# Six of eight gated head outputs turned by VectorE block transposes and a trip through DRAM, with the first output pair's last quad of inputs taken at its end

## The reference, cut to what matters

```python
o = o * lax.rsqrt(jnp.mean(jnp.square(o), axis=-1, keepdims=True) + RMS_EPS)
o = o.reshape(B, S, H * dv) * gn.astype(jnp.float32)
gate = jax.nn.silu((h @ wg).astype(jnp.float32))
return (gate * o).astype(h.dtype) @ wo
```

## Time and profile before

| | |
|---|---|
| median of three executions | 2486.74 us |
| lowest and highest | 2486.59 and 2487.62 us |
| the profiled execution's own time | 2487.13 us |
| its span in the trace | 2485.3 us |
| PE, DVE, ACT, POOL busy | 2474.5, 1915.0, 1402.3, 158.6 us |
| retention in the trace | from about 1084 to 1802 us |
| its output pairs | 1358.96 to 1444.22 and 1717.19 to 1802.45 us |
| granted TensorE clock | 0.999 of full speed |

### The profile page before, as it was taken

How to read it: one execution, slowest core, us unless ns; L and a number is a source line. 1 busy time by engine, 2 the same in 40 slices (tenths; PEclk the granted TensorE clock), 3 DMA queues, 4 the chain that set the end, 5 groups by cost and what they waited for, 6 DMA issues and landing times.

```text
span 2485.3 us, 30031 instructions
## 1 busy us (share of the span) xinstructions
PE 2474.5 (100%) x11128; PEld 2050.7 (83%) x11128; DVE 1915.0 (77%) x2118; ACT 1402.3 (56%) x1689; POOL 158.6 (6%) x272
## 2 busy tenths in 40 slices
PE   9999999999999999999999999999999999999998
PEld 7888888888888888888888888888888888888887
DVE  6455555887978888987778868778988888788787
ACT  7454445554646555655556545656565555464564
POOL 0000000100100000101110001000010000010010
PEclk9999999999999999999999999999999999999999
DMA  8445456675756766766665665666677666666584
GB/s 312 158 155 182 140 200 218 214 253 182 260 202 222 248 208 229 237 212 204 219 225 184 231 201 183 199 206 233 236 248 245 207 231 229 211 237 237 192 273 146
DMA packets 148503, 534.83 MB, mean 215 GB/s; under 512 B 18704, under 2 KB 18960, under 8 KB 147472
## 3 DMA queue, kind: packets, MB, share of 16 engines
q1 hardware_dynamic: 131040, 476.65, 55.1%
q0 software_dynamic: 17184, 56.11, 7.9%
q10 hardware_dynamic: 144, 0.26, 0.0%
HBM read 506.74 MB, written 26.21 MB: 214 GB/s over the span
## 4 chain that ended last, share of the span: by engine, by line
PE 53%; DVE 2%; issue 1%; DMA 1%; ACT 1%; POOL 0%; DVEq 0%; ACTq 0%; POOLq 0%
PE acc L905 9%; PE acc L907 9%; PE acc L906 9%; PE sc L907 7%; PE sc L906 7%; PE sc L905 7%; PE mix L906 1%; PE mix L907 1%; PE mix L905 1%; DVE w_lo L1916 1%; ACT w_hi L1339 0%; DMA raw<-in_w_stream 0%; DMA evac<-park 0%; PE tr L1054 0%; PE tr L703 0%
## 5 line engine op out<-in xcount | busy, mean ns | idle before, releaser
L1916 DVE TENSOR_TENSOR w_lo<-raw,w_hi 128x1024 fp32r<-128x1024 f32 x696 | 847.1, 1230 | 290.4 <-ACT w_hi L1339 287.8
L1339 ACT ACTIVATE w_hi<-raw 128x1024 fp32r<-128x1024 f32 x696 | 727.8, 1058 | 571.8 <-PE sc L907 185.3
L905 PE MATMUL acc<-w_hi,xT_hi 128*128 128x512 f32 x826 | 322.6, 391 | 1.0 <-DVE xT_lo L1981 0.6
L907 PE MATMUL acc<-w_hi,xT_lo 128*128 128x512 f32 x826 | 321.6, 389 | 0.0
L906 PE MATMUL acc<-w_lo,xT_hi 128*128 128x512 f32 x826 | 321.5, 389 | 0.0
L1339 ACT ACTIVATE w_hi<-scratch 128x1024 fp32r<-128x1024 f32 x201 | 211.8, 1057 | 169.3 <-PE acc L907 74.4
L1916 DVE TENSOR_TENSOR w_lo<-scratch,w_hi 128x1024 fp32r<-128x1024 f32 x201 | 244.7, 1220 | 68.1 <-ACT w_hi L1339 67.5
L905 PE MATMUL sc<-w_hi,xT_hi 128*128 128x512 f32 x736 | 287.4, 390 | 0.0
L907 PE MATMUL sc<-w_hi,xT_lo 128*128 128x512 f32 x736 | 286.6, 389 | 0.0
L906 PE MATMUL sc<-w_lo,xT_hi 128*128 128x512 f32 x736 | 286.4, 389 | 0.0
L905 PE MATMUL acc<-w_hi,aT_hi 128*128 128x512 f32 x600 | 233.8, 390 | 0.0
(11 more groups left out here) (279 smaller groups left out, 3930.5 us busy)
## 6 DMA issues: line engine op xcount, KB each, us to landing
raw<-in_w_stream SPq DMA_DIRECT2D x725, 512.0 KB, 4.6
scratch<-in_w_stream SPq DMA_DIRECT2D x171, 512.0 KB, 4.8
park<-stage POOLq DMA_DIRECT2D x38, 512.0 KB, 3.2
evac<-park POOLq DMA_DIRECT2D x152, 128.0 KB, 3.2
gain<-in_gains POOLq DMA_DIRECT2D x4, 1024.0 KB, 8.1
qk_park<-evac POOLq DMA_DIRECT2D x8, 512.0 KB, 4.8
scratch<-qk_park POOLq DMA_DIRECT2D x32, 128.0 KB, 5.3
h<-in_x SPq DMA_DIRECT2D x2, 1024.0 KB, 8.7
```

The source lines that it names most:

```text
L905: pe.matmul(bank[:, :], x_hi, w_hi[:, c], start=start, stop=False, skip_group_check=True)
L907: return pe.matmul(bank[:, :], x_lo, w_hi[:, c], start=False, stop=stop, skip_group_check=True)
L1339: act.activation(w_hi[:, slot * SW:(slot + 1) * SW], mlp_raw(u, load_of(u, t)), ACT.Copy).then_inc(mlp_hi, 1)
L1916: dve.tensor_tensor(w_lo[:, c], mlp_raw(u, load_of(u, t)), w_hi[:, c].bitcast(F32), ALU.subtract).then_inc(mlp_lo, 1)
```

## The change

The output of a half's first head still goes through PE. For the second, third and fourth head of each half (`o_turn` counts these six) DVE turns the blocks from `stage` to `evac` (`turn_o_blocks`), POOL parks and fetches (`park_o`, `fetch_o`), ACT makes `aT_hi` in one copy (`high_o`) and DVE `aT_lo` in one subtraction (`low_o`). The second and third heads' outputs are fetched into `stage`, behind the next head's turned queries and keys; the fourth's into `evac`. ACT waits for the park before it puts the next head's queries and keys into `evac`. The first output pair of each half joins `LATE`, so that its tiles on quad 3 (the fourth head's) are the last of each block; before tiles on quads 1, 2 and 3 PE waits for `o_made`.

```diff
-LATE = {mlp_unit(m, i) for m in range(2) for i in range(2, PAIRS, 4)}
+LATE = {mlp_unit(m, i) for m in range(2) for i in range(2, PAIRS, 4)} | {wo_unit(half, 0) for half in range(2)}
...
+            def park_o(hd):
+
+                pool.wait_ge(o_turned, o_turn(hd) + 1)
+                pool.dma_start(o_park[o_turn(hd)], evac_both[:, :]).then_inc(o_parked, 16)
+                pool.wait_ge(o_parked, 16 * (o_turn(hd) + 1))
+
+            def fetch_o(hd, into):
+
+                rows = o_park[o_turn(hd)].rearrange("(a c) (b k) -> b c a k", a=GRID, b=GRID)
+                for g in range(GRID):
+                    pool.dma_start(into[g * TB:(g + 1) * TB, :].rearrange("p (a k) -> p a k", a=GRID),
+                                   rows[g]).then_inc(o_fetched, 16)
...
+                if hd % RET_HALF > 1:
+                    park_o(hd - 1)
                 turn_qk(hd)
+                if hd % RET_HALF > 1:
+                    fetch_o(hd - 1, stage_both)
...
+                if hd % RET_HALF == RET_HALF - 1:
+                    park_o(hd)
+                    fetch_o(hd, evac_both)
             load_gain(2)
+            pool.wait_ge(o_made, O_TURNS)
...
+                    if half == 0 and s % 2 == 0 and outputs is not None:
+                        pe.wait_ge(o_made, outputs + 1 + s // 2)
...
-                    if hd == 0 and s == 2 or hd % RET_HALF and s == 3:
+                    if hd == 0 and s == 2 or hd % RET_HALF == 1 and s == 3:
                         own()
-                    if hd == 0 and s == 3 or hd % RET_HALF and s == 4:
+                    if hd == 0 and s == 3 or hd % RET_HALF == 1 and s == 4:
                         pending()
...
-                    if n == 0 and t == SEVEN:
-                        own()
-                    if n == 0 and t == SEVEN + 1:
-                        pending()
...
+                if hd % RET_HALF > 1:
+                    act.wait_ge(o_parked, 16 * (o_turn(hd - 1) + 1))
                 for t in range(TOKS):
                     act.wait_ge(qk_done[t], hd + 1)
                     act.activation(evac[t][:, :], banks_of(u - 1)[t][:, :], ACT.Copy,
...
+            def high_o(hd):
+                act.wait_ge(o_fetched, GRID * 16 * (o_turn(hd) + 1))
+                tiles = fetched_tiles if hd % RET_HALF == RET_HALF - 1 else staged_tiles
+                act.activation(in_toks_and_tiles(aT_hi, hd % RET_HALF), tiles, ACT.Copy).then_inc(o_hi_made, 1)
...
+            def low_o(hd):
+                dve.wait_ge(o_hi_made, o_turn(hd) + 1)
...
+            def turn_o_blocks(hd):
+
+                for t in range(TOKS):
+                    dve.wait_ge(staged[t], QUADS + SUPER * QUADS + QUADS + hd + 1)
+                dve.transpose(evac_both[:, :].rearrange("p (b m r) -> p m b r", b=GRID, r=TB),
+                              stage_both[:, :].rearrange("p (m b c) -> p m b c", b=GRID, c=TB)).then_inc(o_turned, 1)
```

More of the change, by code:

```diff
@@ L248, with o_turn @@
 STAGED = list_staged()
+def o_turn(hd):
+    return hd // RET_HALF * (RET_HALF - 1) + hd % RET_HALF - 1
+O_TURNS = 2 * (RET_HALF - 1)
 C_ID, C_TRI, C_ONE, C_MASK = 0, P, 2 * P, 3 * P
@@ L407, in in_toks_and_tiles @@
             return quads.rearrange("p t (j a r) -> p t j a r", j=NB // P, a=GRID)
+        staged_tiles = stage_both[:, :].rearrange("p (a t j r) -> p t j a r", a=GRID, t=TOKS, j=NB // P)
         fetched_tiles = evac_both[:, :].rearrange("p (a t j r) -> p t j a r", a=GRID, t=TOKS, j=NB // P)
@@ L432, in build_trunk @@
         staged = pair("staged")
+        o_turned, o_parked, o_fetched, o_hi_made, o_made = (
+            sem(name) for name in ("o_turned", "o_parked", "o_fetched", "o_hi_made", "o_made"))
         rotated_made, qk_turned, qk_parked, qk_fetched, qk_made = (
@@ L490, in build_trunk @@
         park = nc.dram_tensor("park", (TURNS, P, TOKS * NB), F32, kind="Internal").ap()
+        o_park = nc.dram_tensor("o_park", (O_TURNS, P, TOKS * NB), F32, kind="Internal").ap()
         qk_park = nc.dram_tensor("qk_park", (RET_HEADS, P, TOKS * NB), F32, kind="Internal").ap()
@@ L965, in seven_pair @@
             def seven_pair(u, lhs, between, turned=False, after_block=False, heads_done=0, end=False, first_turn=None,
-                           turns=0):
+                           turns=0, outputs=None):
                 unit, up = UNITS[u], lhs is xT
@@ L1103, in between @@
                 def between(t):
-                    if n == 0 and t == SEVEN:
-                        own()
-                    if n == 0 and t == SEVEN + 1:
-                        pending()
-                seven_pair(wo_unit(half, n), aT, between, turned=n == 0, heads_done=(half + 1) * RET_HALF)
+                    pass
+                if n == 0:
+                    skip_staged(RET_HALF - 1)
+                seven_pair(wo_unit(half, n), aT, between, heads_done=(half + 1) * RET_HALF,
+                           outputs=half * (RET_HALF - 1) if n == 0 else None)
             for half in range(2):
@@ L1465, in seven_pair @@
                 if was_head:
+                    high_o(hd - 1)
                     squares_of_o(hd)
@@ L1508, in seven_pair @@
                 hi(u, 12)
-                if was_head:
-                    batch_hi(0, aT_hi, QUADS - 1)
-                    batch_hi(1, aT_hi, QUADS - 1)
                 if new_sums and not late_norm:
@@ L1520, in seven_pair @@
                 hi(u, 15)
+                if was_head:
+                    high_o(hd)
                 if late_norm and new_sums:
@@ L1569, in query_key_block @@
                     hi(u, 1)
+                    if hd % RET_HALF == RET_HALF - 1:
+                        high_o(hd - 2)
                     hi(u, 2)
@@ L1595, in value_gate_pair @@
                 hi(u, TAU1)
-                if hd % RET_HALF:
+                if new_sums:
                     batch_hi(0, turned, quad)
                 hi(u, TAU3)
-                if hd % RET_HALF:
+                if new_sums:
                     batch_hi(1, turned, quad)
@@ L2030, in gated_out @@
                 dve.tensor_tensor(stage[tok][:, :], evac[tok][:, :], gate_r[tok], ALU.mult).then_inc(staged[tok], 1)
+            def low_o(hd):
+                dve.wait_ge(o_hi_made, o_turn(hd) + 1)
+                tiles = fetched_tiles if hd % RET_HALF == RET_HALF - 1 else staged_tiles
+                hi_part, lo_part = (in_toks_and_tiles(part, hd % RET_HALF) for part in (aT_hi, aT_lo))
+                dve.tensor_tensor(lo_part, tiles, hi_part.bitcast(F32), ALU.subtract).then_inc(o_made, 1)
             def u_part(u, parts):
@@ L2095, in seven_pair @@
                     gained_after(1, p_quad, z_out, done)
+                if was_head:
+                    low_o(hd - 1)
                 lo(u, B21)
@@ L2134, in seven_pair @@
                     gated_out(hd, 1)
+                    turn_o_blocks(hd)
                 lo(u, 9)
@@ L2153, in seven_pair @@
                     norm_for_mlp()
-                if was_head:
-                    batch_lo(0, aT_hi, aT_lo, QUADS - 1)
-                    batch_lo(1, aT_hi, aT_lo, QUADS - 1)
                 lo(u, 13)
@@ L2167, in seven_pair @@
                 lo(u, 15)
+                if was_head:
+                    low_o(hd)
                 if late_norm and new_sums:
@@ L2257, in query_key_block @@
                     lo(u, 1)
+                    if hd % RET_HALF == RET_HALF - 1:
+                        low_o(hd - 2)
                     lo(u, 2)
@@ L2274, in value_gate_pair @@
                 new_sums = hd % RET_HALF == 1
-                turns = hd % RET_HALF and not new_sums
                 lo(u, B11)
@@ L2283, in value_gate_pair @@
                     gated_out(hd - 1, 1)
+                if hd % RET_HALF > 1:
+                    turn_o_blocks(hd - 1)
                 tau13(u)
@@ L2286, in value_gate_pair @@
                 tau2(u)
-                if turns:
-                    batch_lo(0, *turned, quad)
                 lo(u, TAU3)
-                if turns:
-                    batch_lo(1, *turned, quad)
                 if new_sums:
```

## The result

The changed kernel takes 2496.97 us in the median of six executions (2494.32 to 2499.15) against 2487.18 for the kernel before on the same chip: the ratio is 1.0039, 95% interval 1.0026 to 1.0052. It is slower by 9.8 us; the prediction said 2481.5, faster, and its range ended at 2485.2. The profiled execution is the fastest of the six.

A forecast was written before the change was run, and what follows sets the result against it. PE, busy 2474.5 of 2485.3 us, was taken to bound the kernel. Saved transposes -5.64, fourth heads' waits +0.3 and normalisation +0.1 gave -5.2 us: from the median 2486.74 to 2481.5 us, range 2480.6 to 2485.2.

The forecast's parts named there:

- PE's saving: Query-key units and first output pairs: six heads lose two transpose batches each, 0.94 us per head, 5.64 us in all.
- I cost these edits at nothing; the cover is idle time: Second and third heads: added DVE, ACT and POOL work costs zero, as DVE is busy 77% and ACT 56%.
- rival 3: Weight loads: new DRAM traffic holds them up, some 2.5 us lost in each of six heads, 2496 us; chance 0.08.
- The threshold of 8.6 us per load: Weight loads: with four raw slots PE's pace of 2.72 us a tile holds until a load takes 8.6 us.
- The second point of the fourth head's chain: Bank-freeing addition for the second output pair, behind more DVE work: between 2.3 us to spare and 1.3 us late.
- the fourth head's two chains: First output pairs: fetched output split before tile 15, and bank freed for the next pair; 0.3 us, bounds 0 and 2.6.
- The trip itself: Park of 512 KB and four fetches through DRAM, read from the queries' and keys' trips: 12.6 to 15.2 us.
- The normalisation term: Behind the second half: first turned quad split three tiles later; zero to 0.6 us, taken as 0.1.
- the one of the Trainium skill on transposes: Transpose 128 x 128 on TensorE where PSUM will do, VectorE for 32 x 32; by it about 1 us slower; not followed.
- the sum of engine work: Six heads: 1.1 us more on DVE less 0.94 us off PE each, about 1 us slower in all; not followed.
- The estimate of 7 to 9 us for a trip: Park and fetch: about 2.0 us plus bytes at 436 KB per us each; set aside for the longer times in the rows.

The follow-up runs named there:

- skip_six: Kernel before without the transposes of the second, third and fourth heads' outputs, nothing in their place, old tile order (not the reference's output): 2481.39 us.
- late_mid: Changed kernel with the fourth head's output back on PE's transposes; second and third heads over DRAM, new tile order in both halves: 2492.30 us.
- late_only: Kernel before with only the new tile order of both halves' first output pairs; every output still through PE: 2490.24 us.
- late_half0: Kernel before with the new tile order in half 0's first output pair alone: 2487.80 us.
- mid_tiny: Changed kernel with the fourth head by PE, old tile order, and the middle heads' transfers cut to four rows (not the reference's output): 2484.42 us.
- wait_only: Changed kernel with the fourth head's trip made of five 16 KB transfers in a row (not the reference's output): 2501.60 us.
- gain_early: Changed kernel with the next norm's 1 MB gain load issued behind the second head, not behind the fourth head's fetch: 2496.24 us.

## Why the prediction was wrong

**PE's saving was right.** 5.64 us were forecast; `skip_six` measured 5.7, and the query-key units have the forecast 21.76 us.

**"I cost these edits at nothing; the cover is idle time"** was wrong for the middle heads. The trips' instructions and waits took 0.8 us for four heads and their bytes 2.8, all of these heads' gain. I had dismissed rival 3 because the queries' and keys' trips make the same traffic without a wait; the new trip comes on top of that one, at the same time. That rival 3's 2496 is close to the measured time is luck: it put 2.5 us into each of six heads, and the profile has 0 to 1.1 in the heads and 10.8 at half 1's end. Its sign, waits of ACT for weight loads well above 108 us, is weak too: 108.4 before, 115.6 after. The threshold of 8.6 us per load wasn't needed either: waits of 0.8 to 2.9 us for single loads reach PE where a chain, here that of the values, has no more lead.

**The second point of the fourth head's chain was seen and mis-sized.** The wait for the freed bank is there as described (1.73 us at 1759.02, forecast 0 to 1.3), and so is the chain ahead of it (13.3 us from `low_o`'s end, forecast 12.2 to 13.2). The step that failed is to stop at that one wait: the addition is also the start of a row of DVE that PE overtakes, and in half 1 the next pair pays 4.1 us for it. For the fourth head's two chains I took 0.3 with a bound of 2.6. Against `late_mid` the changed kernel loses 9.79 - 4.70 = 5.1 us more although it saves 1.9 more on PE: about 7 us. The trip itself was within its bounds (13.58 and 15.24 us).

**The normalisation term, 0.1 with a bound of 0.6,** was 2.9 us by `late_only`, if `late_half0`'s 0.7 counts as none. I had looked at the moved instructions and not at the units behind, where the delay meets PE's own batch in the MLP's first pair (2.2 us there in `late_only`'s windows, 4.4 in the changed kernel's) and, once the lead is gone, the second output pair.

**The sum in its place,** from distances of medians: batches -5.7, middle heads' trips +3.6, tile order +2.9, fourth heads' trips +7, which gives +7.8. The measured +9.8 is 2 us more. `late_mid` shows about as much: +4.7 where its parts give 0.1 + 2.9. These costs aren't independent, since all draw on the same lead; how the 2 us divide stays open. Half 0's first pair alone differs by 2.4 us between profiles.

Of the two rules, the one of the Trainium skill on transposes (VectorE: DVE Perf Modes, Rules for kernel authors) pointed the right way, but not by the sum of engine work: `mid_tiny` has the block transposes and subtractions of four heads and gives back 0.8 us. (That sum's 1.1 us already held the 1.24 us of the block transpose; the prediction's sentence names them side by side.) The estimate of 7 to 9 us for a trip by the Trainium skill (DMA: Bandwidth & Descriptors, Anatomy of one DMA) is not what the trace shows: 13.58 and 15.24 us. The same page of the Trainium skill (Queues, rings and completion order) says that a DMA engine takes turns between the queues that have work. The rows agree: with POOL's queue busy beside SP's, a weight load goes from 4.4 to 9.0 us.

## What to carry to other kernels

Price a trip through DRAM by the loads that it slows as well as by its own length; the test is a run with the same instructions and short transfers. In a program with fixed order, an engine's wait costs the lead of all that stands behind it, and the bill comes a unit later: follow it until the lead is back. What it comes to depends on the rows there: behind the same wait half 0's next pair lost 0.1 to 0.2 us and half 1's 4.1. Leaving the old work out with nothing in its place tells cheaply what a change can win at most.

## What the hardware showed

After PE's wait of 1.9 us that ended at 1814.82 the granted clock fell to half, 1.2 GHz, and was back at 2.4 GHz before 1820. Windows of the changed kernel:

```profile
1814.00:1816.00 2.00, 1.18 (x7) 1.09 (x8) 2.00 (x4) 1.79 (x4) 0.00 (x0) 0.95 0.97 274
1816.00:1818.00 2.00, 2.00 (x6) 1.54 (x6) 1.69 (x3) 2.00 (x5) 0.00 (x0) 0.50 1.02 408
1818.00:1820.00 2.00, 2.00 (x10) 1.58 (x9) 2.00 (x2) 2.00 (x3) 0.00 (x0) 0.70 0.83 279
1820.00:1830.00 10.00, 10.00 (x47) 8.30 (x46) 9.90 (x15) 6.70 (x8) 0.00 (x0) 1.00 0.83 287
```

The first three windows lack 0.05, 0.50 and 0.30 of 2 us at full clock, 1.7 us together, behind a wait of 1.9. In `wait_only` and `gain_early` PE stood for 1.9 us at the same tile (until 1822.39 and 1816.65), and the granted clock of that pair stayed at 1.00.
